# RWKV pairs of a hybrid block: decay and rate as half-row products between the masked scores of two chunks, ahead of the keys

## The reference

```python
r, k, v, g, w_lo, a_lo = jnp.split(h, list(np.cumsum(widths)[:-1]), axis=-1)
w = -jax.nn.softplus(-(w0 + jnp.tanh(w_lo) @ w2)) - 0.5     # decay
a = jax.nn.sigmoid(a0 + a_lo @ a2)                          # rate
kk = (k * k_k); kk = kk / jnp.maximum(norm(kk), 1e-12)
k = k * (1 + (a - 1) * k_a)
decay = jnp.exp(-jnp.exp(w))
y = _wkv7_scan(r, decay, k, v, -kk, kk * a)                 # recurrence over the tokens
bonus = jnp.sum(r * k * r_k, axis=-1, keepdims=True) * v
```

## Time and profile before

| | |
|---|---|
| median of 3 runs | 1562.4 us (1561.64 to 1563.75) |
| profiled execution | 1561.25 us, its span 1559.4 us |
| TensorE busy | 1503.5 us, 96% of the span |
| VectorE busy | 985.0 us, 63% |
| ScalarE busy | 842.2 us, 54% |
| chain that ended last | TensorE 86%, VectorE 6%, ScalarE 5% |

### The profile page before, as it was taken

The page is one execution under the profiler, slowest core; times in us unless marked ns, Lnnn a source line. Parts: engine busy times, 40 slices in busy tenths (PEclk is TensorE's granted clock), DMA queues, the critical chain, the costliest instruction groups (busy, mean ns, idle before and its releaser), DMA issues.

```text
span 1559.4 us, 26786 instructions
## 1 busy us (share of the span) xinstructions
PE 1503.5 (96%) x10524; PEld 1326.2 (85%) x10524; DVE 985.0 (63%) x1881; ACT 842.2 (54%) x2044; POOL 50.4 (3%) x28
## 2 busy tenths in 40 slices
PE   7999899999999999899899999999999999999997
PEld 7598777888889999788788889888898877789986
DVE  3367468454338886687777777777777413666764
ACT  3265433444237775546566666666666424555553
POOL 1143100000000000000000000000000000000000
PEclk9999999999999999999999999999999999999999
DMA  9364323121335555413110111101111035333331
GB/s 370 119 226 138 109 88 108 58 78 55 135 135 191 188 190 189 136 59 131 55 55 29 55 55 55 55 30 54 55 55 55 28 108 206 132 109 118 126 118 45
DMA packets 25820, 167.75 MB, mean 108 GB/s; under 512 B 3680, under 2 KB 5088, under 8 KB 6112
## 3 DMA queue, kind: packets, MB, share of 16 engines
q1 hardware_dynamic: 24512, 164.93, 30.1%
q10 hardware_dynamic: 1184, 1.11, 0.2%
HBM read 164.99 MB, written 1.05 MB: 106 GB/s over the span
## 4 chain that ended last, share of the span: by engine, by line
PE 86%; DVE 6%; ACT 5%; issue 2%; DMA 1%; DVEq 0%; SPq 0%; ACTq 0%
PE bank L747 8%; PE bank L748 8%; PE bank L749 8%; PE bank L731 5%; PE bank L1090 4%; PE bank L1073 4%; PE bank L878 3%; PE bank L824 3%; PE bank L1240 3%; PE bank L1224 3%; PE bank L1103 3%; PE bank L1075 2%; PE bank L1074 2%; PE bank L761 2%; PE bank L1217 1%
## 5 line engine op out<-in xcount | busy, mean ns | idle before, releaser
L660 DVE TENSOR_TENSOR ring_lo<-ring,w_hi_rw 128x1024 fp32r<-128x1024 f32 x117 | 142.7, 1222 | 38.8 <-ACT w_hi_rw L1504 37.6
L660 DVE TENSOR_TENSOR w_lo<-ring,w_hi 128x1024 fp32r<-128x1024 f32 x80 | 100.6, 1261 | 83.4 <-ACT w_hi L1504 82.4
L1504 ACT ACTIVATE w_hi_rw<-ring 128x1024 fp32r<-128x1024 f32 x117 | 122.6, 1051 | 51.9 <-PE bank L749 30.9
L1472 ACT ACTIVATE arena<-bank 128x272 f32<-128x272 f32 (+2 forms) x165 | 66.8, 406 | 129.5 <-PE bank L749 41.7
L1073 PE MATMUL bank<-x_hi,w_hi_rw 128*128 128x272 f32 x384 | 135.0, 352 | 0.1
L1504 ACT ACTIVATE w_hi<-ring 128x1024 fp32r<-128x1024 f32 x98 | 103.1, 1056 | 19.1 <-PE bank L749 15.0
L1075 PE MATMUL bank<-x_hi,ring_lo 128*128 128x272 f32 x384 | 110.8, 288 | 0.0
L1074 PE MATMUL bank<-x_lo,w_hi_rw 128*128 128x272 f32 x384 | 110.7, 288 | 0.0
L747 PE MATMUL bank<-u_hi,w_hi 128*128 128x256 f32 x320 | 90.8, 284 | 1.4 <-DVE w_lo L660 1.4
L748 PE MATMUL bank<-u_lo,w_hi 128*128 128x256 f32 x320 | 90.5, 283 | 0.0
L749 PE MATMUL bank<-u_hi,w_lo 128*128 128x256 f32 x320 | 90.5, 283 | 0.0
(11 more groups left out here) (487 smaller groups left out, 4307.0 us busy)
## 6 DMA issues: line engine op xcount, KB each, us to landing
ring<-wstream SPq DMA_DIRECT2D x151, 1024.0 KB, 4.9
con<-consts SPq DMA_DIRECT2D x1, 2400.0 KB, 15.1
h<-xT SPq DMA_DIRECT2D x1, 1024.0 KB, 6.1
arena<-wlora ACTq DMA_DIRECT2D x1, 1024.0 KB, 4.8
out<-arena SPq DMA_DIRECT2D x4, 256.0 KB, 2.5
arena<-decays SPq DMA_DIRECT2D x2, 384.0 KB, 5.4
gain_post<-gains SPq DMA_DIRECT2D x1, 512.0 KB, 5.7
arena<-decays SPq DMA_DIRECT2D x1, 256.0 KB, 5.6
```

The source lines that it names most:

```text
L660: ops.tensor_tensor(lo, whole, hi.bitcast(F32), ALU.subtract).then_inc(S(signal), 1)
L1472: nc.scalar.activation(out, bank[i % 2][rows_, 0:n], func, **kw).then_inc(S("proj_taken"), 1)
L1504: nc.scalar.activation(hi, whole, ACT.Copy).then_inc(S("w_hi_ready"), 1)
```

## The change

Decay and rate move to the front of the order in every pair. Their product reads 64 rows each of `wl` and of a single `lo`, without zeros. A new slot `low_rank` of two blocks stands between the scores of chunk 1 and those of chunk 2; the slots `grams` and `first` have one block less each. ScalarE's `tanh_table()` moves ahead of the bonus, and `square_key` follows the keys directly and waits for them alone. The two memsets of `lo` on GpSimd go.

```diff
-R_K, R_W, R_A, R_R, R_KK, R_V, R_BONUS = range(7)
-RW_OUTS = (8, 1, 1, 8, 1, 8, 1)
+R_W, R_A, R_K, R_R, R_KK, R_V, R_BONUS = range(7)
+RW_OUTS = (1, 1, 8, 8, 1, 8, 1)
-FILL = {"start": 1, "bonus": 1, "grams": 5, "gram0": 4, "first": 3}
+FILL = {"start": 1, "bonus": 1, "low_rank": 2, "grams": 4, "gram0": 4, "first": 2}
...
-        lo = area(taken[0], 2, T2)
+        lo = area(taken[0], T2)
...
                     if j in (R_W, R_A):
-                        ins = nc.tensor.matmul(b[:, 0:T2], wl[:, q * P:(q + 1) * P], lo[:, j - R_W, :], start=True, stop=True)
+                        r = slice(64 * (j - R_W), 64 * (j - R_W) + 64)
+                        ins = nc.tensor.matmul(b[:, 0:T2], wl[r, q * P:(q + 1) * P], lo[r, :], start=True, stop=True)
...
                 grams(p, 1)
+                fill(fill_end(p, "low_rank"))
                 grams(p, 2)
                 fill(fill_end(p, "grams"))
...
-                act.wait_ge(S("proj_taken"), taken_n[0] - (q > 0))
+                act.wait_ge(S("proj_taken"), taken_n[0])
...
                     take(gin[:, q % 2, 2, :], n=T2)
-                    if q == 0:
-                        square_key(q)
+                    square_key(q)
...
-                    if j == R_W and q > 0:
-                        square_key(q)
...
                 if p >= 2:
                     deviation(p - 2)
+                tanh_table()
                 take_until(fill_end(p, "bonus"))
-                tanh_table()
+                take_until(fill_end(p, "low_rank"))
                 split_rw(p + 1, R_V)
...
-            nc.gpsimd.memset(lo[64:128, 0, :], 0.0).then_inc(S("lo_zeroed"), 1)
-            pool.wait_ge(S("lo_zeroed"), 1)
-            nc.gpsimd.memset(lo[0:64, 1, :], 0.0).then_inc(S("lo_zeroed"), 1)
```

More of the change, by code:

```diff
@@ L162, in outs_at @@
     q, r = divmod(n, sum(RW_OUTS))
[L163 to L169, removed]
+    return len(RW_OUTS) * q + sum(1 for i in range(len(RW_OUTS)) if sum(RW_OUTS[:i + 1]) <= r)
 def rw_at(q, j):
-    return len(RW_OUTS) * q + list(rw_order(q)).index(j)
+    return len(RW_OUTS) * q + j
 CONV_FROM = (8, 0, 16)
@@ L461, in build @@
         wl = area(taken[0], INNER)
-        lo = area(taken[0], 2, T2)
-        assert taken[0] == XG_LO
+        lo = area(taken[0], T2)
+        assert taken[0] <= XG_LO
         cs, dd, Wc, kk2, sdk, kp = [area(XG_LO + i * T2, T2) for i in range(6)]
@@ L1047, in fill @@
                     q, k = divmod(filled[0], sum(RW_OUTS))
-                    for j in rw_order(q):
+                    for j in range(len(RW_OUTS)):
                         if k < RW_OUTS[j]:
@@ L1830, in _ @@
                     taken_n[0] += 1
-                    act.wait_ge(S("lo_zeroed"), 2)
-                    nc.scalar.activation(lo[0:64, 0, :], bank[i % 2][0:64, 0:T2], ACT.Tanh)
-                    nc.scalar.activation(lo[64:128, 1, :], bank[i % 2][64:128, 0:T2], ACT.Copy).then_inc(S("proj_taken"), 1)
+                    nc.scalar.activation(lo[0:64, :], bank[i % 2][0:64, 0:T2], ACT.Tanh)
+                    nc.scalar.activation(lo[64:128, :], bank[i % 2][64:128, 0:T2], ACT.Copy).then_inc(S("proj_taken"), 1)
                     round_x(4)
@@ L1881, in take_until @@
                     q, i = divmod(took[0], len(RW_OUTS))
-                    take_rwkv(q, rw_order(q)[i])
+                    take_rwkv(q, i)
                     took[0] += 1
@@ L2948, in _ @@
             pool.wait_ge(S("rw_zeroed"), 3)
-            pool.wait_ge(S("proj_done"), 92 + 2 * FT + DT)
-            nc.gpsimd.memset(lo[64:128, 0, :], 0.0).then_inc(S("lo_zeroed"), 1)
-            pool.wait_ge(S("lo_zeroed"), 1)
-            nc.gpsimd.memset(lo[0:64, 1, :], 0.0).then_inc(S("lo_zeroed"), 1)
-            pool.wait_ge(S("lo_zeroed"), 2)
             pool.wait_ge(S("h_tile"), 4 * DT)
@@ L2967, in gemm_sizes @@
     for p in range(PAIRS):
-        n += [DT if RW_OUTS[j] > 1 else 0 for j in rw_order(p)]
+        n += [DT if n_ > 1 else 0 for n_ in RW_OUTS]
     n += [len(m) * (k1 - k0) for m, k0, k1 in OUT_PIECES] + [2 * DT - 1, 1] + [DT] * 5 + [0, 0, 8] * 4
```

## The result

The changed kernel takes 1573.93 us in the median of 4 runs (1572.66 to 1574.29), the kernel before 1563.08 on the same chips (1561.64 to 1564.09). The ratio is 1.0069, 95% interval 1.0055 to 1.0082: slower by 10.8 us. The forecast was 1573, range 1567 to 1579.

What follows compares the result with a forecast made beforehand. TensorE, nearly always busy, was taken as the pace of the periodic pairs. Terms of 11.5 - 0.5 - 0.2 = +10.8 us on 1562.4 gave 1573.2, stated as 1573, range 1567 to 1579.

Steps and rivals of the forecast that it cites:

- The wait at the rate: Pairs 2 to 14: TensorE's rate product waits 0.58 us until ScalarE, after the table load, has taken the bonus.
- what overlaps: Pairs 2 to 14: nothing runs side by side; chunk 2's scores start 0.46 + 0.11 us after the rate's start.
- +1.23: Pairs 2 to 14: scores of chunk 0 late by 1.61 us, minus 0.375 for one key block fewer ahead.
- What ScalarE gives back: Pairs 2 to 14, after the turned scores: token copies end sooner, so chunk 0's transposes regain 0.35 us.
- The two ends of the range, 0 and 0.74: ScalarE's relief per pair: nothing (total 1578) or 0.74 us in full (1568); ends of the likeliest case, chance 0.81.
- Net: Each of 13 pairs, 2 to 14: +1.61 - 0.375 - 0.35 = +0.88 us, together +11.5.
- Pairs 0 and 1: No root precedes the load, so no wait: -0.26 us each, -0.5 together; pair 0's products ahead of the loop -0.2.
- No wait at the rate: Rival: bonus taken before the decay is through, -0.26 us in each of 15 pairs, total 1558.3 us; chance 0.08.
- No overlap: Rival: half rows at full price without wait, +0.20 us per pair, 1565 us; chance 0.07 together with around no change.
- The longer load: Rival: the table load delays ScalarE's next activation by 1.28 us more, 1590 us; chance 0.04 including other such delays.

Runs made afterwards that it cites:

- Experiment 1: The changed kernel with ScalarE taking the bonus before the table load, as before the change: 1561.3 us, ratio 0.9984 to the kernel before.
- experiment 2: The kernel before with only the table load moved ahead of the bonus: 1563.23 us, ratio 0.9999 to the kernel before.
- experiment 6: The changed kernel with four small extra activations between table load and bonus: 1580.83 us, ratio 1.0110 to the kernel before.
- Experiment 4: Experiment 1 with one key block moved from behind the scores to ahead of chunk 0's transposes: 1554.74 us, ratio 0.9943 to the kernel before.
- experiment 3: Experiment 1 with whole-row, zero-padded products for decay and rate at the same place: 1572.86 us, ratio 1.0062 to the kernel before.
- experiment 5: The changed kernel with decay and rate behind the scores of both chunks instead of between them: 1570.52 us, ratio 1.0049 to the kernel before.

## Why the prediction was right

**The wait at the rate.** Forecast at 0.58 behind the decay, measured 0.57. The bonus was taken 1.94 behind the start of the scores (forecast 957.67 - 955.71 = 1.96). Experiments 1, 2 and 6 show it as the cause: take it away, and the loss goes; move the load without a product that needs the bank, and nothing happens; lengthen it, and the pair grows by as much.

**The step that was slightly off: what overlaps.** I let the scores of chunk 2 start when the rate was through, 0.46 + 0.11 later. The timeline has their first passes at 961.53, together with the rate's first pass, since one of them uses rows 0 to 63, which the rate leaves free. So the forecast that nothing runs side by side in these pairs was wrong. It gains almost nothing, because rows 64 to 127 still have the rate and four passes of the scores to do: from the rate's start to the keys it is 1.51, against 1.53 forecast (957.72 to 959.25). The keys start 3.50 behind the scores, against 3.54 forecast, and the scores of chunk 0 start 5.21 behind them against 4.01 before, so +1.20 where the sum has +1.23.

**What ScalarE gives back.** Forecast 0.35, since the square must now wait for the keys' own signal. Measured at the transposes of chunk 0: 969.57 - 959.54 = 10.03 against 964.88 - 955.71 = 9.17, so +0.86, of which 1.20 came before: 0.34. The two ends of the range, 0 and 0.74, did not come about. The wait of about 0.5 for token copies was there too: 0.36 in the row's brackets, and 0.52 from the time at which the last pass of r would have let the next one start (968.92 + 0.13 = 969.05). Experiment 4 turned it into a gain.

**Net.** +0.88 forecast, +0.87 measured, in 13 pairs. This is what carries the forecast.

**Pairs 0 and 1.** Forecast -0.26 each and -0.2 ahead of the loop, so -0.7. Measured -0.28 up to the scores of pair 1 and -0.2 in pair 1, so -0.5. Pair 1 bears the forecast out; the share of pair 0 can't be read from these traces. Its bonus starts 1.66 sooner than before (727.24 against 728.90), though experiments 1 and 6, where TensorE has the same program up to there, have 727.06 and 728.47. And 1.38 of that is lost again up to the scores of pair 1, in a trace whose mean granted clock from 727 to 732 was 0.66, where before it was 1.00. That this term came out near is luck.

**What the sum did not contain.** The profiled spans differ by 12.7, not 10.8; the 1.85 behind the pairs were not foreseen. Up to the first product of the next layer the traces differ by 10.85, the forecast's amount. The medians differ by 10.8, within an interval of 2 on either side, so part of the close hit is luck.

**The rivals.** No wait at the rate: only in pairs 0 and 1. Experiment 1, which is this rival made true, is worth 0.9984 and not the 0.9974 that 1558.3 would be, because the keys then wait 0.12 for the decay's bank; the prediction of that rival left this out. No overlap: refuted by pair 1 and experiment 3. The longer load: the bonus begins 0.13 behind the load's end (960.97 to 961.10), and the load itself 0.01 behind the root's (959.68 to 959.69). The Trainium skill (ScalarE: Activation LUTs, What ACT_TABLE_LOAD costs) puts about 1380 ns of drain beside the load; this trace has none on either side of it.

## What to carry to other kernels

With two result banks in turn, an output waits for the one two places before it. Moving an output earlier thus moves a wait onto whatever the other engine does ahead of that take; look there for long steps such as a table load. Check both engines' orders together: the load and the new place were each harmless by themselves and cost 0.9 us a pair together. And where a stall remains on the path, give the engine a block from a place where it is not short of work: moving one key block was worth 6.6 us.

## What the runs showed of the hardware

**The granted clock cost 1.7 us behind the pairs.** Behind the pairs TensorE stands idle for 2.81 us, in both kernels, until the first product of the next layer. Timelines of TensorE there, before and after:

```profile
1309.40 2.99 PE L1286 MATMUL bank<-u,ring 128*128 128x272 f32 x12 [2.81 <-ACT u L2034]
```

```profile
1320.25 4.68 PE L1283 MATMUL bank<-u,ring 128*128 128x272 f32 x12 [2.81 <-ACT u L2028]
```

Busy time by stretch (PE, PEld, DVE, ACT, POOL, then the granted clock, the DMA share and GB/s) of the stretch with these twelve passes, before and after:

```profile
1309.40:1312.20 2.80, 2.80 (x12) 2.36 (x13) 2.65 (x4) 2.80 (x9) 0.00 (x0) 1.00 1.01 421
```

```profile
1320.20:1324.80 4.60, 4.55 (x13) 3.49 (x14) 3.80 (x6) 4.60 (x13) 0.73 (x1) 0.63 0.66 274
```

The same twelve passes with the same idle before them took 1.69 longer, at a mean granted clock of 0.63, that is mostly at 1.2 instead of 2.4 GHz. TensorE had the same work ahead of the idle in both. All eight traces have this idle of 2.81: the twelve passes took 2.99 in those of before and of experiments 2 and 5, 4.62 to 4.68 in those of the changed kernel and of experiments 1 and 6, and 5.78 in those of experiments 3 and 4. What decides it is open. The place in the execution alone does not: the passes start at 1318.09 in experiment 3 and at 1318.27 in experiment 5. Nothing ties it to the change either: experiment 5 has all of the change but one step of the order, and kept the full clock.

The times of the kernel before follow the mean granted clock. In its 21 executions beside experiments 1 to 4, the five at 0.992 took 1560.73 to 1562.20 us, the six at 0.991 1563.13 to 1563.88, and the nine at 0.990 1564.08 to 1564.87. Those of experiment 1 hardly do: from 0.990 to 0.993 they lie within 1.5 us. So a difference of 0.1% between single executions or single traces of such kernels can be the clock's; the periods of the pairs are the firmer measure, since the granted clock from 794 to 1160 was 1.00 in both traces.

**Half rows overlap across different products.** The rate's passes and a pass of the scores, in other rows and another bank, start at the same time (961.53). The Trainium skill (TensorEngine Tiling (Array Packing), Key Properties) says that tiles operate independently; the trace agrees for products that belong to different steps as well.
